# Index keys projected ahead of the index queries, a row ring of six, and an output projection prepared in the block before it

## The chip, the core and the metric

The kernel runs on one core of a Trainium2 chip. Its engines work from instruction streams of their own: TensorE (PE, matrix products), VectorE (DVE), ScalarE (ACT), GpSimd (POOL) and SyncE (SP, which here only issues transfers). Semaphores order them against each other. The metric is the device time of one execution in microseconds (us).

## The reference, cut to what matters

One inference step of one decoder layer, for a prompt of 1024 tokens and 8 samples of 4 tokens, with D_MODEL = 1024:

```python
mod = silu(c) @ w_ada + b_ada                       # six vectors per sequence: sh1, sc1, g1, sh2, sc2, g2
xn = rms_norm(x, norm1_g) * (1 + sc1) + sh1
qa, ka, va, qb, kb, vb, iq, ik, iw = split_proj(xn @ w_in)
# q, k of both mixers: rms_norm and rotary; iq, ik: rotary only
oa = combine_patterns(dilated attention of 8 heads under three (window, dilation) patterns)
I = sum_h iw[:, h] * relu(iq[:, h] @ ik.T)          # 8 index heads of 64
sel = top_k(I, 256 causal keys per query);  ob = softmax attention of 8 heads over sel
x = x + g1 * (concat(oa, ob) @ w_out)
xn = rms_norm(x, norm2_g) * (1 + sc2) + sh2
y = x + g2 * ((silu(gate) * up) @ w_down)           # gate, up = split(xn @ w_gate_up)
```

## The kernel before

The program is four blocks in sequence; all engines meet at the end of each: `front` (norm, modulation, input projection, index scores, top-k search), `attention` (prompt), `sample_attention` (the samples' attention) and `back` (output projection, second norm, FFN). Tokens stand in columns in three thirds of 352 (1024 + 32 samples), or in nine tiles of rows (eight of 128 and one of 32). Products in fp32 are made in three passes: a high and a low part of each operand (whi, wlo of the weights, xhi, xlo of the normed input), as hi x hi, hi x lo and lo x hi, each a group of eight matmuls over the depth of 1024. ACT writes the high parts, POOL the low parts of weights, DVE those of x.

**Projection.** `project` takes a chunk of up to 256 columns of w_in and runs its nine units (one for each row tile). The index chunks stand first (CH, L307: iq, iq, ik), then the index scores (`indexer`), then nine late chunks (LATE, L308: qa, qa, ka, ka, kv, qb, qb, va, va). The key chunk ik of 128 columns is projected the other way round, into three thirds (L613, 72 products in all), copied out by ACT as ikF, and turned into nine row tiles (L634); ACT copies out each tile's keys (ikn) and head weights (iw), POOL rotates them. Then come `kk` (the keys rounded, ACT L903) and `ll` (their remainder, POOL L1106), PE's transposes of both (L686), and `turn_queries` (L691) for each head. A pass over x starts with DVE's normed xnorm (L1217 to L1233) and its remainder xlo (L1237).

**Late chunks.** ACT's `unit` (L836) copies a unit out of PSUM into a row of `ubuf`, a ring of four, and sums squares per head; `root` (L830) takes the root of the sum of the unit before; DVE scales the row (L1442), POOL rotates it, and SP stores it to memory. A row is free once its store has landed (L851). Between units DVE runs the search for the top-k thresholds, for which ACT makes some of the counts (`tally`). After each of the late chunks except the last, two pieces of the modulation are multiplied (`ada`, L576, eight matmuls of 32 x 256 each); ACT copies each to modn (L809), and `ada_turn` (L590) turns it with two small matmuls behind units 0 and 1 of the next chunk. All engines keep the order in which their code is written.

**Sample attention and back.** `sample_attention` loads window keys kw (8 loads of 512 KB; consts after the first), turns them, ACT and DVE copy them out as kTa (ACT L2148), and so on to PE's last transposes of the result into oT (L2137). `back` then loads the output weights ow (SP `load_out` L2309), ACT rounds oT to ahi (L2473) and ow to owh (L2469), POOL makes owl (L2555), DVE makes alo (L2604), and PE multiplies (L2387).

Of the kernel before, what the change touches and what calls it, by code (L numbers as in the profile page):

```python
# [32 lines left out]
P = 128  # L33
# [27 lines left out]
XB = 25344  # L61

# [132 lines left out]
def front(nc, A, S):  # L195
# [5 lines left out]

    rope = T.at("rope", [P, NTILE + 1, 32], F32, S["pers"])
# [13 lines left out]
    ss = T.at("ss", [P, 4, 4], F32, T.end)  # L216
    sd = T.at("sd", [P, 4, 4], F32, T.end)
    rs = T.at("rs", [P, 4, 4], F32, T.end)
# [23 lines left out]
    ubuf = T.at("ubuf", [P, 4, WCH], F32, UB)  # L242
    usq = T.at("usq", [P, 4, WCH], BF16, T.end)
# [21 lines left out]
    sco = T.at("sco", [P, sum(width)], F32, T.end)  # L265
    relu = T.at("relu", [P, 2, 1024], F32, WB)
    kk = T.at("kk", [P, NTILE, 2, HD], F32R, T.end)
    ll = T.at("ll", [P, NTILE, 2, HD], F32R, T.end)
    qst = T.at("qst", [P, 2, 6, 2, HD], F32R, T.end)
    assert T.end <= WB + 24 * KD * P  # L270
# [36 lines left out]
    CH = [("iq", IQ, 256), ("iq", IQ + 256, 256), ("ik", PROJ - P, P)]  # L307
# [29 lines left out]
    LOAD_AT = 7  # L337
    FIRST_SPLIT_AT = 4
# [51 lines left out]
    tot = [0] * 4  # L390
    for u in range(NIDX, len(units)):
        tot[u % 4] += len(stores(u))
        nst[u] = tot[u % 4]
# [38 lines left out]
    unit_st = [sem(f"unit_st{r}") for r in range(4)]  # L432
# [41 lines left out]
    with nc.Block() as block:  # L474

        @block.sync
        def _(sp):
# [29 lines left out]
            def store(u):  # L507
# [6 lines left out]
                for s in stores(u):  # L514
                    if len(s) == 4:
                        n = s[3]
                        src = ubuf[n * TSEQ:(n + 1) * TSEQ, u % 4, s[1]:s[2]]
                    else:
                        src = ubuf[0:rows, u % 4, s[1]:s[2]]
                    sp.dma_start(s[0], src).then_inc(unit_st[u % 4], 16)  # L520
# [21 lines left out]
        def _(pe):  # L542
# [58 lines left out]
            def project(n, turns=()):  # L601
# [5 lines left out]
                if order[n][0] == "ik":  # L607
                    pe.wait_ge(sx_ev, 2)

                    for th in range(3):  # L610
                        for p, (a, b) in enumerate(((whi, xhi), (wlo, xhi), (whi, xlo))):
                            for k in range(KD):
# [4 lines left out]
                for t in range(NTILE + 1):  # L617
                    u = c * (NTILE + 1) + t
                    if c == 0:
                        th = min(2, (t * P + P - 1) // THIRD)  # L620
                        pe.wait_ge(xhi_done, KD * (th + 1) + (th == 2))
                    if t == 0:
                        pe.wait_ge(ada_nat, ada_at)
                        pe.wait_ge(ada_done, ada_at)
# [12 lines left out]
                    for p, (a, b) in enumerate(((xhi, whi), (xhi, wlo), (xlo, whi))):  # L637
                        if c == 0 and p == 2:
                            pe.wait_ge(xlo_done, KD * (th + 1) + (th == 2))
# [4 lines left out]
                    if t < len(turns):  # L644
                        ada_turn(turns[t])
# [31 lines left out]
            def indexer():  # L677

                pe.wait_ge(ada_done, ada_at)
                for x in range(4):  # L680
                    src, ready = ((kk, 1), (ll, 2))[x // 2]
                    pe.wait_ge(ik_split, ready)
                    if x >= 2:
                        wait_out(pe, x - 2)
# [6 lines left out]
                def turn_queries(h):  # L691
                    pe.wait_ge(iq_hi, h + 1)
                    pe.wait_ge(iq_lo, h + 1)
                    for part in range(2):
                        x = 4 + 2 * h + part
                        wait_out(pe, x - 2)
                        for j in range(4 if part == 0 else 2):
                            mm = pe.transpose(bank[2 + x % 2][:, j * P:(j + 1) * P],
                                              qst[:, h % 2, 4 * part + j].rearrange("p a d -> p (a d)").bitcast(F32),
                                              ident[:])  # L700
                        mm.then_inc(tr_fill, 1)

                turn_queries(0)
# [89 lines left out]
        def _(act):  # L793
# [36 lines left out]
            def root(u):  # L830
                if u >= 0 and normed(u):
                    act.wait_ge(unit_read, u + 1)
                    act.activation(sd[:, u % 4, 0:heads(u)], ss[:, u % 4, 0:heads(u)], ACT.Sqrt,
                                   scale=1.0 / HD, bias=EPS).then_inc(sd_ready, 1)

            def unit(u):  # L836
# [12 lines left out]
                else:  # L849
                    if u - NIDX >= 4:  # L850
                        act.wait_ge(unit_st[u % 4], 16 * nst[u - 4])  # L851
                    last = act.activation(ubuf[:, u % 4, :], src[:, 0:256], ACT.Copy)
                    if normed(u):
                        for h in range(heads(u)):
                            cols = slice(h * HD, (h + 1) * HD)
                            last = act.activation(usq[:, u % 4, cols], src[:, cols], ACT.Square,
                                                  accum_out=ss[:, u % 4, h:h + 1])
# [29 lines left out]
            act.wait_ge(x_spilt, 16)  # L887
            for u in range(9):
                unit(u)
            split_w(base + 2)  # L890
            for u in range(9, 18):
                unit(u)
            for th in range(3):
                act.wait_ge(ikf_mm, th + 1)
                act.activation(ikF[:, th * THIRD:(th + 1) * THIRD],
                               wide[th // 2][:, 512 * (th % 2):512 * (th % 2) + THIRD], ACT.Copy).then_inc(ikf_out, 1)
            for u in range(18, 27):
                unit(u)


            act.wait_ge(unit_rope, rope_before[NIDX])
            act.wait_ge(unit_mm, NIDX)
# [1859 lines left out]
```

## Time and profile before

| | us |
|---|---|
| median of 3 runs (lowest to highest) | 1792.56 (1792.12 to 1794.27) |
| the profiled execution | 1792.48 |
| its span, first to last instruction | 1790.9 |
| PE busy | 1612.7 (90%) |
| DVE, ACT, POOL busy | 868.3, 684.2, 587.3 |

The mean clock that TensorE was granted is 0.954 of full speed. Where the chunks of the projection, the index scores and the blocks lie in the span is read from lines of code: index chunks 72 to 145 us, index scores 158 to 219, late chunks 219 to 522, `attention` to 828, `sample_attention` to 881, `back` to the end. A row of the timeline gives a start, a duration, the engine, the line, what is written and read, how many instructions stand together, and in brackets the idle time ahead of it with what ended it. In rows of waits the columns are total, times and longest.

### The profile page before, as it was taken

What the parts mean: (1) busy time and instruction counts of PE and PEld (TensorE: products, weight loads), DVE (VectorE), ACT (ScalarE), POOL (GpSimd) and SP (SyncE); (2) the same over time, 40 slices, a digit from 0 to 9 for tenths busy, and PEclk for the clock granted to TensorE, in tenths of its full rate; (3) what the DMA queues carried; (4) which work ended last, traced back from release to release, by engine and by line L of the source; (5) the groups of instructions that cost most, each with busy time, mean ns of one, the idle gap of its engine ahead of it and who ended that gap; (6) DMA issues with size and microseconds to landing.
All of it is one profiled execution on the core that took longest, in us unless ns stands there. A gap on an engine that the chain in (4) does not pass through costs nothing.

```text
span 1790.9 us, 29669 instructions
## 1 busy us (share of the span) xinstructions
PE 1612.7 (90%) x10750; PEld 1515.3 (85%) x10750; DVE 868.3 (48%) x1995; ACT 684.2 (38%) x1780; POOL 587.3 (33%) x741
## 2 busy tenths in 40 slices
PE   5696898999888888886699699999999999999998
PEld 3594688888877777775499599999999999999998
DVE  1904977877778888885521731321312313303214
ACT  4414647667437778773322511111121121121111
POOL 2344155646423433212124233232232132232220
PEclk7798999999989999998799899999999999999999
DMA  7700033443342221103530221121011111111002
GB/s 253 260 25 6 25 99 102 129 152 102 111 144 70 86 69 58 38 8 115 218 115 13 66 75 48 36 59 47 23 51 43 47 47 47 47 47 35 12 1 98
DMA packets 138045, 135.30 MB, mean 76 GB/s; under 512 B 7229, under 2 KB 126957, under 8 KB 137302
## 3 DMA queue, kind: packets, MB, share of 16 engines
q1 hardware_dynamic: 111190, 106.43, 18.8%
q10 hardware_dynamic: 25104, 24.64, 4.3%
q0 software_dynamic: 1648, 2.89, 0.5%
q8 instruction: 59, 0.97, 0.2%
q14 instruction: 44, 0.36, 0.1%
HBM read 115.29 MB, written 27.04 MB: 79 GB/s over the span
## 4 chain that ended last, share of the span: by engine, by line
PE 48%; DVE 2%; DMA 1%; ACT 1%; POOL 0%; issue 0%; DVEq 0%; SPq 0%
PE bank L2408 28%; PE wide L2424 14%; PE bank L2387 5%; DVE xn L2647 0%; DVE alo L2657 0%; DMA out_y_p<-yn 0%; DVE rstd L2631 0%; DMA ow<-in_w_out 0%; ACT ahi L2524 0%; POOL owl L2555 0%; DVE yn L2701 0%; ACT gwh L2482 0%; PE wide L2369 0%; PE bank L2448 0%; ACT L2496 0%; ACT L2514 0%
## 5 line engine op out<-in xcount | busy, mean ns | idle before, releaser
L2668 DVE TENSOR_TENSOR hf<-bank,sg 128x352 f32<-128x352 f32 x66 | 34.7, 525 | 463.7 <-PE bank L2408 454.5
L2569 POOL TENSOR_TENSOR hlo<-hf,hhi 128x352 fp32r<-128x352 f32 x66 | 62.7, 949 | 503.9 <-ACT hhi L2498 503.9
L2408 PE MATMUL bank<-ahi,gwh 128*128 128x352 f32 x1056 | 196.3, 328 | 11.5 <-DVE hf L2668 6.6
L2681 DVE SCALAR_TENSOR_TENSOR x<-wide,modT,x 128x352 f32<-128x352 f32 (+1 forms) x264 | 151.2, 573 | 97.0 <-PE wide L2424 97.0
L2408 PE MATMUL bank<-alo,gwh 128*128 128x352 f32 x1056 | 192.1, 324 | 2.3 <-DVE alo L2657 2.3
L2408 PE MATMUL bank<-ahi,gwl 128*128 128x352 f32 x1056 | 193.2, 325 | 0.0
L2408 PEld LDWEIGHTS bank<-ahi,gwh 128*128 128x128 f32 x1056 | 176.3, 190 | 14.3 <-DVE hf L2668 6.9
L2408 PEld LDWEIGHTS bank<-alo,gwh 128*128 128x128 f32 x1056 | 174.2, 189 | 2.9 <-DVE alo L2657 2.9
L2408 PEld LDWEIGHTS bank<-ahi,gwl 128*128 128x128 f32 x1056 | 175.9, 190 | 0.0
L2424 PE MATMUL wide<-hlo,dwh 128*128 128x352 f32 x528 | 171.3, 325 | 0.0
L2424 PE MATMUL wide<-hhi,dwl 128*128 128x352 f32 x528 | 170.4, 323 | 0.0
L2424 PE MATMUL wide<-hhi,dwh 128*128 128x352 f32 x528 | 170.0, 322 | 0.0
L2496 ACT ACTIVATE sg<-bank 128x352 f32<-128x352 f32 x66 | 30.7, 466 | 355.7 <-PE bank L2408 355.7
L2498 ACT ACTIVATE hhi<-hf 128x352 fp32r<-128x352 f32 x66 | 33.0, 500 | 255.9 <-DVE hf L2668 255.9
L2559 POOL TENSOR_TENSOR gwl<-gw,gwh 128x2048 fp32r<-128x2048 f32 x22 | 103.0, 4680 | 62.0 <-ACT gwh L2482 62.0
L1784 PE MATMUL bank<-ident,prob 128*128 128x128 f32 x576 | 97.0, 278 | 17.9 <-DVE pL L1924 17.0
L1924 DVE TENSOR_TENSOR pL<-bank,pH 128x512 fp32r<-128x512 f32 (+1 forms) x192 | 101.3, 551 | 13.4 <-ACT pH L1871 11.7
L1356 DVE TENSOR_SCALAR_CACHE_REDUCE junk<-sig,cand 128x384 uint8<-128x384 f32 (+4 forms) x155 | 106.3, 743 | 0.1
L1896 ACT ACTIVATE prob<-smx,nmax 128x128 f32<-128x128 f32 (+7 forms) x128 | 99.0, 773 | 10.3 <-DVE nmax L1954 9.6
L1871 ACT ACTIVATE pH<-bank 128x512 fp32r<-128x512 f32 (+1 forms) x192 | 90.4, 486 | 25.1 <-PE bank L1784 24.2
L2424 PEld LDWEIGHTS wide<-hhi,dwh 128*128 128x128 f32 x528 | 100.0, 189 | 0.0
L2424 PEld LDWEIGHTS wide<-hlo,dwh 128*128 128x128 f32 x528 | 99.2, 188 | 0.0
(349 smaller groups left out, 3449.1 us busy)
## 6 DMA issues: line engine op xcount, KB each, us to landing
gw<-in_w_gate_up SPq DMA_DIRECT2D x44, 512.0 KB, 5.0
raw<-in_w_ada ACTq DMA_DIRECT2D x14, 1024.0 KB, 6.3
dw<-in_w_down SPq DMA_DIRECT2D x22, 512.0 KB, 3.6
raw<-in_w_ada SPq DMA_DIRECT2D x10, 1024.0 KB, 7.5
raw<-in_w_in ACTq DMA_DIRECT2D x8, 1024.0 KB, 5.4
scr_x<-xT SPq DMA_DIRECT2D x1, 4224.0 KB, 18.6
xnat<-in_x_prompt SPq DMA_DIRECT2D x8, 512.0 KB, 5.8
scr_q<-ubuf SPq DMA_DIRECT2D x32, 128.0 KB, 1.8
```

The lines of the kernel that those rows point to most:

```text
L1356: link(v.tensor_scalar(junk[0:r, joff[a]:joff[a] + w], sig[0:r, o:o + w], cand[0:r, a:a + 1].bitcast(F32), 0.0, ALU.is_ge, ALU.add, accum_ ...
L1784: mm = pe.transpose(dst[:, (j - 4 * b) * P:(j - 4 * b + 1) * P], prob[:, a % RING, j * P:(j + 1) * P], ident[:])
L1871: act.activation(pH[g][:, 4 * b:4 * b + nb, i % 4, :], src[:, 0:nb * P].rearrange("p (j n) -> p j n", n=P), ACT.Copy).then_inc(act_out, 1)
L1896: act.activation(prob[:, m % RING, 0:L], smx[:, m % 2, 0:L], ACT.Exp, scale=-1.0, bias=nmax[:, m % 4:m % 4 + 1], accum_out=rowsum[:, m // ...
L1924: v.tensor_tensor(pL[g][:, 4 * b:4 * b + nb, i % 4, :], src[:, 0:nb * P].rearrange("p (j n) -> p j n", n=P), pH[g][:, 4 * b:4 * b + nb, i ...
L2387: mm = pe.matmul(pb[u % 4][:, 0:THIRD], a[:, d % 2, k, :], b[:, k, third(th)], start=(p == 0 and k == 0), stop=(p == 2 and k == KD - 1))
L2408: mm = pe.matmul(pb[2 * s + side][:, 0:THIRD], a[r][:, k, side, :], b[:, k, third(th)], start=(p == 0 and k == 0), stop=(p == 2 and k == K ...
L2424: mm = pe.matmul(pb[4 + u % 4][:, 0:THIRD], a[:, r, d * P:(d + 1) * P], b[:, r, third(th)], start=(r == 0 and p == 0), stop=(r == 1 and p ...
L2559: pool.tensor_tensor(gwl[r][:], gw[r][:], gwh[r][:].bitcast(F32), ALU.subtract).then_inc(gw_lo, 1)
L2569: pool.tensor_tensor(hlo[:, r, third(th)], hf[:, (3 * r + th) % 2, :], hhi[:, r, third(th)].bitcast(F32), ALU.subtract).then_inc(h_lo, 1)
L2668: v.tensor_tensor(hf[:, s, :], pb[2 * s + 1][:, 0:THIRD], sg[:, s, :], ALU.mult).then_inc(h_mul, 1)
L2681: ins = v.scalar_tensor_tensor(out=x1[:, d, cols], in0=src[:, 0:n], scalar=modT[:, 40 + d, 0:1], in1=x1[:, d, cols], op0=ALU.mult, op1=ALU ...
```

## The change

Three parts.

First, CH becomes ik, iq, iq. The key chunk's products wait for xhi and xlo by thirds, as the first chunk's units did. The kk turns follow the first unit of the second iq chunk, the ll turns the third, and the first head's queries the seventh; they are in a buffer of their own, q0st. ACT makes kk after the fifth unit of the first iq chunk and POOL ll after its rotation; kk, ll and q0st move to where the scores will lie. In ACT and POOL the steps move with them.

Second, ubuf, ss, sd and rs have six rows (ROWS), and `ada_turn` and ACT's bias step stand behind units 3 and 4 (MOD_TURN_AT).

Third, `sample_attention` issues its constants ahead of the window keys, and takes over from `back`: the first two column blocks of ow are loaded, rounded (ACT) and split (POOL) there; ACT rounds two thirds of oT, two pieces after each kTa, and POOL makes their remainders (16 subtractions, olo in place on oT). `back` does the last third. It loads x first, and the down weights only after the output projection.

The core of the diff:

```diff
-    CH = [("iq", IQ, 256), ("iq", IQ + 256, 256), ("ik", PROJ - P, P)]
+    CH = [("ik", PROJ - P, P), ("iq", IQ, 256), ("iq", IQ + 256, 256)]
+    ROWS = 6
-    ubuf = T.at("ubuf", [P, 4, WCH], F32, UB)
+    ubuf = T.at("ubuf", [P, ROWS, WCH], F32, UB)
+    MOD_TURN_AT = 3
...
                     for th in range(3):
+                        pe.wait_ge(xhi_done, KD * (th + 1) + (th == 2))
                         for p, (a, b) in enumerate(((whi, xhi), (wlo, xhi), (whi, xlo))):
+                            if p == 2:
+                                pe.wait_ge(xlo_done, KD * (th + 1) + (th == 2))
...
-                    if t < len(turns):
-                        ada_turn(turns[t])
+                    if 0 <= t - MOD_TURN_AT < len(turns):
+                        ada_turn(turns[t - MOD_TURN_AT])
+                    if c == 2 and t in (0, 2):
+                        turn_keys(t // 2)
+                    if c == 2 and t == 6:
+                        turn_queries(0)
...
-                    if u - NIDX >= 4:
-                        act.wait_ge(unit_st[u % 4], 16 * nst[u - 4])
+                    if u - NIDX >= ROWS:
+                        act.wait_ge(unit_st[u % ROWS], 16 * nst[u - ROWS])
...
-                        if turns:
+                        if turns and t >= MOD_TURN_AT:
                             ada_bias(turns.pop(0))
...
+            sp.wait_ge(sc, 2)
+            for d in range(2):
+                sp.dma_start(ow[:, d], A["w_out"][0, :, d * P:(d + 1) * P].rearrange("(k p) n -> p k n", p=P)
+                             ).then_inc(ow_in[d], 16)
...
+            for th in range(2):
+                for k in range(KD):
+                    pool.wait_ge(o_hi, KD * th + k + 1)
+                    pool.tensor_tensor(olo[:, k, third(th)], oT[:, k, third(th)], ahi[:, k, third(th)].bitcast(F32),
+                                       ALU.subtract).then_inc(o_lo, 1)
+            for d in range(2):
+                pool.wait_ge(ow_hi, d + 1)
+                pool.tensor_tensor(owl[:, d], ow[:, d], owh[:, d].bitcast(F32), ALU.subtract).then_inc(ow_lo, 1)
...
+                for k in (2 * (n % 4), 2 * (n % 4) + 1):
+                    act.activation(ahi[:, k, third(n // 4)], oT[:, k, third(n // 4)], ACT.Copy).then_inc(o_hi, 1)
...
-            load_out(0)
-            load_out(1)
             for g, (k0, k1) in enumerate(XG):
                 sp.dma_start(x1[:, k0:k1], A["scr_x"][:, k0:k1]).then_inc(x_in[g], 16)
             load_out(2)
             load_out(3)
 
-            sp.wait_ge(o_hi, 3 * KD)
-            sp.wait_ge(o_lo, 3 * KD)
             load_gate_up(0, 0)
-            load_down(0, 0)
-            load_down(1, 1)
             for d in range(4, KD):
                 load_out(d)
             sp.wait_ge(op_mm, 3 * KD)
             load_gate_up(1, 1)
+            load_down(0, 0)
+            load_down(1, 1)
```

PE around the index chunks, before: the last unit of the second query chunk, the key chunk's last third (L613) and its turns (L634), then the turns of kk, ll and the queries (L686, L698) and the first score (L719).

```order
L641 MATMUL bank<-whi,xlo 128x256 x8
...
L613 MATMUL wide<-xlo,whi 128x352 x8
L634 MATMUL bank<-ident,ikF 128x128 x8
L634 MATMUL bank<-ident,ikF 32x128
L686 MATMUL bank<-ident,kk 128x128 x8
L686 MATMUL bank<-ident,ll 128x128 x8
L698 MATMUL bank<-ident,qst 128x128 x6
L719 MATMUL wide<-ikH,iqT 128x384
```

PE now: the key chunk (L624) stands first, its turns (L639) next, and the turns of kk, ll (L691) and q0st (L704) lie between units (L644) of the second query chunk.

```order
L624 MATMUL wide<-xlo,whi 128x352 x8
L639 MATMUL bank<-ident,ikF 128x128 x8
L639 MATMUL bank<-ident,ikF 32x128
L644 MATMUL bank<-whi,xhi 128x256 x8
...
L691 MATMUL bank<-ident,kk 128x128 x8
...
L691 MATMUL bank<-ident,ll 128x128 x8
...
L704 MATMUL bank<-ident,q0st 128x128 x6
...
L726 MATMUL wide<-ikH,iqT 128x384
```

The turns moved from behind the last product to between products; the first score follows the last unit.

PE at the start of the second late chunk, before: the two pieces of the modulation (L586), a unit of three groups (L641), and behind it the first turn (L597).

```order
L586 MATMUL bank<-raw,cT 32x256 x16
L641 MATMUL bank<-whi,xhi 128x256 x8
L641 MATMUL bank<-wlo,xhi 128x256 x8
L641 MATMUL bank<-whi,xlo 128x256 x8
L597 MATMUL wide<-modsel,modn 128x9 x2
```

PE now, at the same place: four units (L644) stand between the pieces (L592) and the first turn (L603).

```order
L592 MATMUL bank<-raw,cT 32x256 x16
L644 MATMUL bank<-whi,xhi 128x256 x8
L644 MATMUL bank<-wlo,xhi 128x256 x8
...
L644 MATMUL bank<-wlo,xhi 128x256 x8
L644 MATMUL bank<-whi,xlo 128x256 x8
L603 MATMUL wide<-modsel,modn 128x9 x2
```

The turn moved back by three units.

POOL at the end of the samples' block and the start of the next, before: the last gather of values (vpg), the change of block, and the remainders of four blocks of ow.

```order
L2050 DMA vpg<-in_cache_v 128x128
L2021 UNCONDITIONAL_BRANCH
L2550 UNCONDITIONAL_BRANCH
L2555 TENSOR_TENSOR owl<-ow,owh 128x1024 x4
L2579 TENSOR_TENSOR sqsum<-sqsum,sq_13638 128x352 x3
```

POOL now, from the last gather on: 16 remainders of oT and two of ow stand ahead of the change of block.

```order
L2088 DMA vpg<-in_cache_v 128x128
L2094 TENSOR_TENSOR olo<-oT,ahi 128x352 x16
L2098 TENSOR_TENSOR owl<-ow,owh 128x1024 x2
L2056 UNCONDITIONAL_BRANCH
L2585 UNCONDITIONAL_BRANCH
L2590 TENSOR_TENSOR owl<-ow,owh 128x1024 x2
```

Half of the first four owl moved into the samples' block, behind sixteen new subtractions.

## Rows read from the trace of the kernel before

**Rows 1.** The page: chain that ended last, shares of the span by line.

```profile
PE bank L2408 28%; PE wide L2424 14%; PE bank L2387 5%; DVE xn L2647 0%; DVE alo L2657 0%; DMA out_y_p<-yn 0%; DVE rstd L2631 0%; DMA ow<-in_w_out 0%; ACT ahi L2524 0%; POOL owl L2555 0%; DVE yn L2701 0%; ACT gwh L2482 0%; PE wide L2369 0%; PE bank L2448 0%; ACT L2496 0%; ACT L2514 0%
```

**Rows 2.** Windows: late chunks, samples; PE, PEld, DVE, ACT, POOL busy, clock, DMA.

```profile
219.00:522.00 303.00, 278.07 (x2324) 265.82 (x2323) 237.74 (x661) 179.34 (x803) 155.40 (x333) 0.94 0.36 115
829.00:889.00 60.00, 37.63 (x316) 24.59 (x315) 26.11 (x81) 12.76 (x28) 12.05 (x20) 0.74 0.60 203
```

**Rows 3.** Timeline of PE, index chunks and the turns behind them.

```profile
86.44 1.12 PE L641 MATMUL bank<-whi,xlo 128*128 128x256 f32 x8
87.40 1.12 PE L641 MATMUL bank<-whi,xhi 128*128 128x256 f32 x8
...
140.81 1.44 PE L613 MATMUL wide<-xlo,whi 128*128 128x352 f32 x8
...
145.13 0.29 PE L634 MATMUL bank<-ident,ikF 128*32 128x128 f32 x1 [0.19 <-ACT iw L847]
151.42 1.94 PE L686 MATMUL bank<-ident,kk 128*128 128x128 f32 x8 [6.01 <-ACT kk L903]
```

**Rows 4.** Timeline of DVE, first normed pieces and the last of xlo.

```profile
66.83 4.62 DVE L1217 TENSOR_TENSOR xnorm<-xnorm,sc 128x256 f32<-128x256 f32 x1
71.49 0.43 DVE L1220 TENSOR_TENSOR xnorm<-xnorm,modT 128x256 f32<-128x256 f32 x1
...
90.83 1.01 DVE L1237 TENSOR_TENSOR xlo<-xnorm,xhi 128x320 fp32r<-128x320 f32 x2
```

**Rows 5.** Timeline of ACT: the first relu of the index scores.

```profile
158.38 1.07 ACT L939 ACTIVATE relu<-wide 128x384 f32<-128x384 f32 x2 [0.45 <-PE wide L719]
```

**Rows 6.** Waits of PE, late chunks (218 to 522 us).

```profile
PE wide L597 <- ACT modn L809: 21.0, 6, 5.6
PE bank L586 <- ACT modn L809: 3.5, 1, 3.5
```

**Rows 7.** Waits of ACT on stores of the row ring, same stretch.

```profile
ACT ubuf L852 <- DMA scr_q<-ubuf: 23.2, 6, 6.7
ACT ubuf L852 <- DMA out_win_k_p<-ubuf: 13.9, 5, 4.9
```

**Rows 8.** Timeline of PE, a late chunk: a wait and what follows.

```profile
292.19 1.02 PE L597 MATMUL wide<-modsel,modn 128*128 128x9 f32 x4 [4.72 <-ACT modn L809]
293.06 2.05 PE L641 MATMUL wide<-whi,xhi 128*128 128x256 f32 x8
294.91 1.91 PE L641 MATMUL wide<-wlo,xhi 128*128 128x256 f32 x8
```

**Rows 9.** Waits of DVE, late chunks.

```profile
DVE rs L1439 <- ACT sd L833: 38.1, 21, 3.5
DVE nok L1363 <- ACT tally L969: 19.6, 14, 4.6
```

**Rows 10.** Chain that ended last, output projection: start, duration, what.

```profile
881.10 4.12 DMA ow<-in_w_out
...
885.24 1.07 ACT owh L2469
...
886.38 2.35 POOL owl L2555
```

**Rows 11.** Timeline of PE, samples' block and start of the output projection.

```profile
835.48 2.28 PE L2070 MATMUL bank<-mask_sb,expand 32*128 32x288 f32 x4 [5.86 <-DMA headsel<-in_headsel]
...
888.82 2.68 PE L2387 MATMUL bank<-ahi,owh 128*128 128x352 f32 x8 [8.45 <-POOL owl L2555]
```

**Rows 12.** The page's groups: a POOL subtraction of 128x352 (busy, mean ns).

```profile
L2569 POOL TENSOR_TENSOR hlo<-hf,hhi 128x352 fp32r<-128x352 f32 x66 | 62.7, 949 | 503.9 <-ACT hhi L2498 503.9
```

**Rows 13.** Timeline of DVE, samples' block: the first scaling of pr_s.

```profile
860.07 0.37 DVE L2196 TENSOR_SCALAR pr_s<-pr_s,rsum_s 128x288 f32<-128x288 f32 x1
```

**Rows 14.** Lines L1442 and L1042, late chunks: ns min/median/max.

```profile
L1442 DVE TENSOR_TENSOR ubuf<-ubuf,rs x63: 291/426/2389, 227.7 to 467.6; 128x256 f32<-128x256 f32 x54, 128x128 f32<-128x128 f32 x9
...
L1042 POOL TENSOR_TENSOR wlo<-raw,whi x16: 2397/2411/2588, 237.2 to 479.7; 128x1024 fp32r<-128x1024 f32 x16
```

More of the change, by code:

```diff
@@ L689, in indexer, with turn_queries @@
                     mm.then_inc(tr_fill, 1)
[L691 to L703, printed above, removed]
+            def turn_queries(h):
+                pe.wait_ge(iq_hi, h + 1)
+                pe.wait_ge(iq_lo, h + 1)
+                src = q0st if h == 0 else qst[:, h % 2]
+                for part in range(2):
+                    x = 4 + 2 * h + part
+                    wait_out(pe, x - 2)
+                    for j in range(4 if part == 0 else 2):
+                        mm = pe.transpose(bank[2 + x % 2][:, j * P:(j + 1) * P],
+                                          src[:, 4 * part + j].rearrange("p a d -> p (a d)").bitcast(F32),
+                                          ident[:])
+                    mm.then_inc(tr_fill, 1)
+            def indexer():
                 n = 0
@@ L886, in _ @@
                                    bias=modT[:, k, 0:1]).then_inc(xhi_done, 1)
[L887 to L902, printed above, removed]
-            act.activation(kk[:], ikn[:, 0:NTILE, :].unsqueeze(2).to_broadcast([P, NTILE, 2, HD]),
-                           ACT.Copy).then_inc(ik_split, 1)
             def iq_high(h):
@@ L1102, in _ @@
             split_w(base + 2)
-            for u in range(9, NIDX):
+            for u in range(9, 9 + 5):
                 rotate(u)
@@ L1995, in sample_attention @@
     rsum = T.at("rsum_s", [P, 4], F32, T.end)
+    kw = T.at("kw", [P, 3, KT, 512], F32, T.end)
+    assert T.end <= OW, T.end
+    kTa = T.at("kTa", [P, 4, 4, NEWW], F32, T.end)
+    kTb = T.at("kTb", [P, 4, NEWW], F32, T.end)
+    assert T.end <= S["loaded"]
+    ow = T.at("ow", [P, 2, KD, P], F32, OW)
+    owh = T.at("owh", [P, 2, KD, P], F32R, T.end)
+    owl = T.at("owl", [P, 2, KD, P], F32R, T.end)
+    T.end = OW
     n_pool = A["cache_k"].shape[1]
@@ L2019, in sample_attention, with third @@
     xt = sem("s_o_turned")
+    ow_in = [sem(f"b_ow_in{r}") for r in range(2)]
+    o_hi = sem("b_o_hi")
+    o_lo = sem("b_o_lo")
+    ow_hi = sem("b_ow_hi")
+    ow_lo = sem("b_ow_lo")
+    S.update(ahi=ahi, olo=olo, ow=ow, owh=owh, owl=owl, ow_in=ow_in, o_hi=o_hi, o_lo=o_lo, ow_hi=ow_hi, ow_lo=ow_lo)
+    def third(t):
+        return slice(t * THIRD, (t + 1) * THIRD)
     with nc.Block() as block:
@@ L2153, in _ @@
                                accum_out=lsum[:, x:x + 1]).then_inc(ex, 1)
+            for d in range(2):
+                act.wait_ge(ow_in[d], 16)
+                act.activation(owh[:, d], ow[:, d], ACT.Copy).then_inc(ow_hi, 1)
         @block.vector
@@ L2229, in back @@
     OT = PERS_END
-    ahi = T.at("ahi", [P, KD, TOK], F32R, OT + 4 * KD * TOK)
-    xn = T.at("xn2", [P, KD, TOK], F32, T.end)
+    ahi, olo, ow, owh, owl = [S[x] for x in ("ahi", "olo", "ow", "owh", "owl")]
+    xn = T.at("xn2", [P, KD, TOK], F32, OT + 8 * KD * TOK)
     alo = T.at("alo", [P, KD, TOK], F32R, OT + 8 * KD * TOK)
@@ L2246, in back @@
     hf = T.at("hf", [P, 2, THIRD], F32, T.end)
-    ow = T.at("ow", [P, 2, KD, P], F32, GW + 24 * P * KD)
-    owh = T.at("owh", [P, 2, KD, P], F32R, T.end)
-    owl = T.at("owl", [P, 2, KD, P], F32R, T.end)
-    assert T.end <= SMALL
+    assert OW == GW + 24 * P * KD
     dw = T.at("dw", [P, 2, D], F32, OT)
@@ L2380, in _ @@
                         pe.wait_ge(x1_done, u - 3)
-                    for p, (a, b) in enumerate(((owh, ahi), (owl, ahi), (owh, alo))):
+                    for p, (a, b) in enumerate(((owh, ahi), (owl, ahi), (owh, olo))):
                         for k in range(KD):
@@ L2469, in split_out @@
                 act.activation(owh[:, d % 2], ow[:, d % 2], ACT.Copy).then_inc(ow_hi, 1)
-            for th in range(3):
-                for k in range(KD):
-                    act.activation(ahi[:, k, third(th)], oT[:, k, third(th)], ACT.Copy).then_inc(o_hi, 1)
-                if th == 0:
-                    split_out(0)
-                    split_out(1)
+            for k in range(KD):
+                act.activation(ahi[:, k, third(2)], oT[:, k, third(2)], ACT.Copy).then_inc(o_hi, 1)
             def split_gate_up(i, r, fresh):
@@ L2600, in _ @@
                                    op0=ALU.add, op1=ALU.mult).then_inc(op_link, 1)
[L2601 to L2605 removed]
+            for k in range(KD):
+                v.wait_ge(o_hi, KD * 2 + k + 1)
+                v.tensor_tensor(olo[:, k, third(2)], oT[:, k, third(2)], ahi[:, k, third(2)].bitcast(F32),
+                                ALU.subtract).then_inc(o_lo, 1)
             for d in range(KD):
```

143 lines of the change are left out of this document (79 added, 64 removed).

## The prediction, made before the changed kernel ran

> **What bounds the kernel now.** I read the chain that ended last first: its two largest lines, 28% and 14% of the span, are TensorE (PE) products of the back block [rows 1], which the change leaves as they are. A gain can only come from stretches where PE waits or runs at its lower clock. Two stand out in the stage windows: the projection chunks, 303 us with PE busy 278 and a granted clock of 0.94, and the attention of the samples, 60 us with PE busy 38 at a clock of 0.74 [rows 2]. A third is the step from the last projected index column to the first index score, which the timelines show as short transposes behind waits [rows 3, 5]. The change touches exactly these three; I cost it as A (index keys first), B (six rows, later turns of the modulation) and C (out projection prepared early).
>
> **A, index keys first.** Before, the key chunk comes last. Its last product ends at 142.25 [rows 3], and a serial chain follows: nine ikF transposes until 145.42, POOL's rotations of nine key tiles, ACT's kk, PE's turn of kk at 151.42 after a wait of 6.01, then ll and the queries, and ACT's first relu of a score at 158.38 [rows 3, 5]. That is 16.1 us behind the last product.
>
> After, I build the end up from the front. The key chunk runs in three thirds, and the last group of each needs eight xlo tiles of its third. VectorE (DVE) ends the last of them at 91.84 [rows 4]. Half as many columns make the first weight split of POOL half as long, which stood before DVE's first step (4.62 us, where the like step behind it takes 0.43 [rows 4]); I let the xlo chain end 2.5 us earlier, at 89.3 (bounds: 0 and 4). The last group of eight, 1.44 [rows 3], gives 90.8. The nine ikF transposes, 3.2 us (142.25 to 145.42), give 94.0. Two query chunks are 18 units of three groups that start 0.96 apart [rows 3], 2.88 each: 51.8, so 145.8. Between their units now stand the turns of kk (1.94 at about half clock [rows 3]), ll and six query transposes, which fall on the full clock: I take 2.5 for all, 148.3. None of them should wait: POOL has a whole chunk (26 us) for its nine key rotations, which took 7 us, and kk and ll behind them. What is left behind the last product is one query tile's copy and rotation, the second head's split and the first score with its relu: 2.5 (the last three are about 1.5 in the chain before; between 1.5 and 4). The first relu stands at 150.8 instead of 158.4: A = **-7.5**. With xlo not earlier and PE at its lower clock for the last third and the first unit after it (4 us), A = -1; with the best ends -10. The index scores go at a pace that DVE and ACT set, so what the first relu gains is passed on whole.
>
> **B, six rows, and the turns at units 3 and 4.** In the chunks PE waits 21.0 + 3.5 = 24.5 us for ACT's modn, the copy that ada_turn turns [rows 6]. ACT has it late because its in-order stream stands at the next unit's ubuf copy until a store of the row four units back has landed; the two larger groups of such waits are 23.2 and 13.9 us [rows 7]. A row's way is copy, squares, a root one unit later, DVE's scale, POOL's rotation, store. Four units are 11.5 us, and since ACT stands for it, the way takes somewhat more; six rows give 17.3. Independently the turn moves behind units 3 and 4, so modn has three more units, 8.6 us, where the longest wait is 5.6 [rows 6]. Either half by itself would cover most of it; both together leave nothing: -24.5.
>
> Each wait also drops the clock. After 4.72 us at 292.19 a group of eight takes 2.05 us against 1.12 [rows 3, 8]; such groups start 1.85 apart and not 0.96, and with three of them after each wait 2.7 us go. Of the seven waits one or two are short and cost less; I take 15.5 for all. B is at most -40. It doesn't have to come whole, since DVE searches the top-k thresholds in the same stretch and the block ends when both do. DVE is busy 237.7 of 303 us [rows 2] and waits 38.1 for ACT's sd and 19.6 for its tally [rows 9]. With PE's 40 us gone 263 are left: DVE would be busy 90%, and its waits would have to shrink from 58 to 25. Most should, since sd and tally are late for the reason that ACT is held, but not surely all; I give back 6. B = **-34**, between -16 (below) and -40. The store waits are ACT's alone, so nothing is queued behind them on another engine; the two added rows are 2 KB of each partition and take no time.
>
> **C, out projection prepared early.** The chain behind the samples' last transposes is: load of ow 4.12, ACT's owh 1.07, POOL's owl 2.35, and PE starts at 888.82 after 8.45 us [rows 10, 11]. After, ow, owh and owl of the first two column blocks and two thirds of ahi and olo are done inside the sample block, where ACT and POOL have little else, and PE starts at about 881.2: -7.6. The last third's eight ahi and olo are due only when PE has done two thirds, 7.7 us later, and are covered. The constants now precede the first key window: PE waited 5.86 us for the last of them [rows 11], issued behind 512 KB; -0.5. Added are 16 subtractions on POOL of about 0.95 each [rows 12], 15 us from the end of its gathers on, in which DVE's four scalings of pr_s (0.37 each [rows 13]) stand on PE's path. The row of 4.62 [rows 4] shows that POOL can hold DVE as long as its own operation lasts; a scaling that meets one loses up to 0.95, and I take two: +1.6. In the back x1 is loaded first and the down weights only behind the out projection. The down products come after a whole pair's gate and up products, over 20 us; I cost that at nothing (uncovered, one load and its split: 6 us). C = **-6.5**, between 0 and -8.5.
>
> The Trainium skill ("SBUF — State Buffer", section "Who interferes with whom") calls that pair of ports a lock: a VectorE operation in a two-port mode, or with two operands in SBUF against a GpSimd operation that reads SBUF, stands until the other is over. The trace agrees (4.62 against 0.43); by that rule POOL's new work could hold only the four scalings, 3.8 us at most, and not the copies out of PSUM around them.
>
> **The sum.** The profiled execution took 1792.48 us with a span of 1790.9; the median is 1792.56, so no correction. 1792.5 - 7.5 - 34 - 6.5 = **1744.5**.
>
> **Rivals.** (1) DVE sets the end of the projection. If its waits on ACT [rows 9] stay for the most part, because latency and not ACT's stall causes them, then PE waits at the end for DVE and little but what DVE spares comes back: B = -16, total 1762.5. For it: 90% busy is close. Against it: ACT's stalls are in the trace. (2) A gives little: the thirds wait for xlo at the lower clock, and the turns inside the second query chunk stand for kk, ll or the query split, each of which needs ACT and POOL in turn; A = -1, total 1751. (3) Half of B only: a new cause (tallies, splits) keeps modn late, B = -20, total 1758.5. (4) Slower than before: POOL and DVE bunch. A scale in the chunks takes 0.43 in the median and 2.39 at most, about as long as one of POOL's wlo splits (2.41) [rows 14]. If the closer stream sets the 54 full-size scales against POOL operations of that length, each takes 1.9 more, 103 us on DVE. DVE has 303 - 238 = 65 us, and A and C give 14: it decides from 79 / 1.9 = 42 of the 54 on, and at all of them the total is 1792.5 + 103 - 79 = 1816. Against it: there are only 16 such splits [rows 14], so POOL's short rotations would have to hold as long.
>
> **How the numbers follow.** The forecast and what lies within 8 us of it: 0.62. Rival 1: 0.14. Rival 3: 0.10. Rival 2: 0.09. Rival 4: 0.02. Several shortfalls at once, near no change: 0.03. The low end is A -10, B -39, C -8.5, or 1735; the high end takes in rivals 2, 3 and 1 with a little margin: 1765. A measurement of this kernel can tell about 0.2%, 3.6 us, from no change; all but 5 in 100 end below 1789.
>
> **What would show it.** A: the first relu at 151 instead of 158, and no 6 us wait before the kk turn. B: no wait for modn over 1 us, ACT's waits on stores under 10 us in all, the granted clock of the chunks at 0.99, and the chunks some 34 us shorter; if DVE's waits on sd stay near 38 instead, rival 1. C: the first product of the out projection within 1 us of the samples' last transpose, and no scaling of pr_s over 1 us. The prediction is wrong if the waits for modn vanish and the end of the projection doesn't come forward by over 20 us.

## The result, and the profile after

The changed kernel takes 1745.36 us in the median (1743.9 to 1747.06), the kernel before on the same chip 1793.41; the ratio is 0.9733, 95% interval 0.9716 to 0.9749. The forecast was 1744.5. The total fits within 1 us, but its three terms don't: by the two profiled executions two came out larger and one much smaller than forecast.

Where the 48.6 us of the two spans (1790.9 to 1742.3) lie, by the starts of the first instruction of each stage in the two traces:

| stage | before | after | gain |
|---|---|---|---|
| start to the first relu of the scores | 158.38 | 152.66 | 5.72 |
| first relu to the first product of the late chunks | 60.43 | 64.10 | -3.67 |
| late chunks, to the last product | 302.79 | 263.11 | 39.68 |
| step into `attention`, and that block | 307.06 | 308.05 | -0.99 |
| samples' block, to the first product of the output projection | 60.16 | 51.82 | 8.34 |
| the rest | 902.1 | 902.6 | -0.5 |

The windows of the changed kernel, for the late chunks, the scores and the samples' block. The columns are length, busy time of PE, its weight loads, DVE, ACT and POOL, the granted clock, and DMA.

```profile
216.76:479.87 263.11, 262.36 (x2326) 252.02 (x2324) 239.64 (x662) 177.91 (x802) 155.95 (x333) 1.00 0.41 132
152.66:216.76 64.10, 48.34 (x212) 34.13 (x212) 54.16 (x54) 40.81 (x63) 16.20 (x10) 0.89 0.02 5
787.92:839.74 51.82, 36.74 (x318) 24.00 (x318) 24.31 (x72) 15.41 (x35) 28.70 (x36) 0.80 0.63 210
```

Against [rows 2]: in the late chunks PE is busy for all but 0.75 us, at the full clock, and DVE is busy for about as long as it was. That is all that the chunks can give while PE does these products. The waits of the same stretch, answering [rows 6, 7, 9] (total, times, longest):

```profile
PE bank L592 <- ACT modn L816: 0.7, 1, 0.7
...
ACT ubuf L859 <- DMA out_win_k_p<-ubuf: 0.9, 1, 0.9
...
DVE rs L1457 <- ACT sd L840: 10.7, 9, 2.6
DVE nok L1381 <- ACT tally L977: 4.2, 5, 1.4
```

The waits for modn fell from 24.5 to 0.7, ACT's waits on stores to 0.9, and DVE's two waits on ACT from 57.7 to 14.9. The chunks end with PE's last product and DVE's last write of the search. The two are level here (479.87 and 479.78), and they were in the kernel before (521.60 and 522.08), so a gain needed both to come earlier. Their rows, before and then after:

```profile
520.56 1.04 PE L660 MATMUL bank<-ident,lst 128*128 128x128 f32 x8
521.78 0.30 DVE L1417 TENSOR_SCALAR mask_sb<-sig 32x288 f32<-32x288 f32 x1
...
478.83 1.04 PE L667 MATMUL bank<-ident,lst 128*128 128x128 f32 x8
479.48 0.30 DVE L1435 TENSOR_SCALAR mask_sb<-sig 32x288 f32<-32x288 f32 x1
```

The start, on PE (answering [rows 3]): the last group of the keys' third, which waits for xlo; the end of the nine turns; the first two groups of queries; the turns between the units; the first score.

```profile
89.96 1.55 PE L624 MATMUL wide<-xlo,whi 128*128 128x352 f32 x8 [2.29 <-DVE xlo L1256]
...
94.39 0.28 PE L639 MATMUL bank<-ident,ikF 128*32 128x128 f32 x1 [0.20 <-ACT iw L854]
94.67 1.64 PE L644 MATMUL bank<-whi,xhi 128*128 128x256 f32 x8
96.10 1.91 PE L644 MATMUL bank<-wlo,xhi 128*128 128x256 f32 x8
...
125.02 1.03 PE L691 MATMUL bank<-ident,kk 128*128 128x128 f32 x8
131.64 1.04 PE L691 MATMUL bank<-ident,ll 128*128 128x128 f32 x8
144.02 0.82 PE L704 MATMUL bank<-ident,q0st 128*128 128x128 f32 x6
...
150.42 0.34 PE L726 MATMUL wide<-ikH,iqT 128*128 128x384 f32 x1
```

No turn waits, as forecast; three turns cost 2.9 (2.5 forecast). The first unit of queries takes 4.4 us from 94.67 to 99.10 where a unit at the full clock takes 2.88.

The scores are where the gain was lost. DVE, POOL and PE in the third head, each from the timeline of that engine:

```profile
169.05 6.78 DVE L1288 SCALAR_TENSOR_TENSOR sco<-relu,iw,sco 128x384 f32<-128x384 f32 x3 [1.31 <-ACT relu L947]
```

```profile
168.72 4.51 POOL L1044 TENSOR_TENSOR wlo<-raw,whi 128x2048 fp32r<-128x2048 f32 x1 [7.11 <-ACT whi L835]
```

```profile
174.59 1.51 PE L704 MATMUL bank<-ident,qst 128*128 128x128 f32 x6 [4.62 <-issue]
175.76 0.78 PE L726 MATMUL wide<-ikH,iqT 128*128 128x512 f32 x1
```

POOL splits the weights of the first late chunk in the middle of the scores. DVE's step stands for as long, PE idles for 4.62 us and goes on at the lower clock (six turns in 1.51 us, against 0.82 above). The kernel before has the same stall, so it was no news of the change; but there PE was back at the full clock by the fourth head, and in this execution of the changed kernel it was not. The windows of that head, of the changed kernel, of the kernel before, and of e1 (below), whose code is the changed kernel's up to there:

```profile
181.96:190.19 8.23, 7.11 (x27) 5.22 (x27) 6.78 (x8) 5.13 (x10) 1.69 (x1) 0.79 0.00 0
```

```profile
185.26:192.25 6.99, 5.76 (x27) 3.84 (x27) 6.75 (x8) 5.02 (x9) 1.69 (x1) 1.00 0.00 0
```

```profile
181.70:188.68 6.98, 5.75 (x27) 3.83 (x27) 6.74 (x8) 5.02 (x10) 1.70 (x1) 1.00 0.00 0
```

So of the 3.67 us 1.2 lie in this head, 1.1 in the third by the same cause (13.42 against 12.31), and 1.3 in the first (7.60 against 6.30), where PE's turn of the second head's queries stands until POOL has made their remainder, which comes behind two transfers of keys (it ends at 155.16):

```profile
155.26 0.84 PE L704 MATMUL bank<-ident,qst 128*128 128x128 f32 x6 [1.17 <-issue]
```

```profile
152.49 0.96 POOL L1130 DMA_DIRECT2D out_ik_p<-ikn  x1 [0.30 <-POOL iqn L1094]
153.45 0.52 POOL L1131 DMA_DIRECT2D out_ik_s<-ikn  x1
153.98 1.18 POOL L1106 TENSOR_TENSOR qst<-iqn,qst 128x384 fp32r<-128x384 f32 x1
```

Only the loss in the first head belongs to the new order. In e1 to e4, which have the changed kernel's code up to there, the first head takes 7.61 to 9.73 us, the third 12.42 to 13.41 and the fourth 6.98 to 7.04; in e8, with the old order, these are 6.30, 13.15 and 6.99. What the third and fourth head lost here differs from execution to execution.

The samples' block: the output projection starts 0.92 us behind the change of block and waits for nothing else (8.45 before, [rows 11]), but one scaling of pr_s takes 2.37 us instead of 0.37 [rows 13], and PE waits for it:

```profile
819.22 2.37 DVE L2247 TENSOR_SCALAR pr_s<-pr_s,rsum_s 128x288 f32<-128x288 f32 x1
```

```profile
807.15 14.28 POOL L2094 TENSOR_TENSOR olo<-oT,ahi 128x352 fp32r<-128x352 f32 x16
```

```profile
821.65 1.35 PE L2159 MATMUL bank<-ident,pr_s 128*128 128x128 f32 x6 [3.82 <-DVE pr_s L2247]
...
839.74 2.68 PE L2426 MATMUL bank<-ahi,owh 128*128 128x352 f32 x8 [0.92 <-PEq L2056]
```

The scaling ends at 821.59, POOL's run of 16 subtractions at 821.43. From that turn of pr_s to the end of the block's last transposes this execution had more of the full clock than the kernel before and the other runs that leave POOL's run whole. The windows of that stretch, before, after, and in e2 (below):

```profile
860.49:880.37 19.88, 17.83 (x140) 9.86 (x140) 6.30 (x18) 0.41 (x2) 0.00 (x0) 0.70 0.21 75
```

```profile
821.65:838.82 17.17, 15.56 (x140) 7.71 (x140) 6.31 (x18) 2.12 (x2) 4.70 (x2) 0.80 0.36 103
```

```profile
817.97:837.70 19.73, 18.33 (x140) 8.39 (x140) 6.30 (x18) 2.12 (x2) 4.67 (x2) 0.67 0.25 65
```

### The profile page after: what moved, and what is told of

It is laid out like the page before. It is cut to its first block, busy times and chain, and to the rows that moved or that the text cites. A ratio compares the mean times of both kernels' runs of the same rounds, so it can differ in the third digit from the quotient of the medians.

```text
span 1742.3 us, 29645 instructions
## 1 busy us (share of the span) xinstructions
PE 1596.6 (92%) x10750; PEld 1502.3 (86%) x10750; DVE 862.1 (49%) x1979; ACT 682.0 (39%) x1780; POOL 601.2 (35%) x757
## 4 chain that ended last, share of the span: by engine, by line
PE 49%; DVE 2%; ACT 1%; DMA 0%; issue 0%; DVEq 0%; ACTq 0%; SPq 0%
PE bank L2447 29%; PE wide L2463 15%; PE bank L2426 5%; DVE xn L2681 0%; DVE alo L2691 0%; DVE rstd L2665 0%; DMA out_y_p<-yn 0%; ACT ahi L2559 0%; PE bank L2487 0%; ACT gwh L2517 0%; PE wide L2408 0%; DVE yn L2735 0%; ACT L2531 0%; ACT L2549 0%; ACT yn L2583 0%
## 5 line engine op out<-in xcount | busy, mean ns | idle before, releaser
L1914 ACT ACTIVATE prob<-smx,nmax 128x128 f32<-128x128 f32 (+7 forms) x128 | 98.7, 771 | 10.4 <-DVE nmax L1972 9.7
L2463 PEld LDWEIGHTS wide<-hhi,dwl 128*128 128x128 f32 x528 | 99.2, 188 | 0.0
```

Source lines behind the costliest of these rows:

```text
L1914: act.activation(prob[:, m % RING, 0:L], smx[:, m % 2, 0:L], ACT.Exp, scale=-1.0, bias=nmax[:, m % 4:m % 4 + 1], accum_out=rowsum[:, m // ...
L2463: mm = pe.matmul(pb[4 + u % 4][:, 0:THIRD], a[:, r, d * P:(d + 1) * P], b[:, r, third(th)], start=(r == 0 and p == 0), stop=(r == 1 and p ...
```

## The experiments

All start from the changed kernel. Its own time is 1745.36. A ratio in brackets is to the kernel before on the same chip, with its 95% interval; the changed kernel's own is 0.9733 (0.9716 to 0.9749).

**e1_ring4 and e2_turn0: which half of B does it?** e1 takes the ring back to four rows, e2 the turns back to units 0 and 1.

```diff
-    ROWS = 6                      (e1)
+    ROWS = 4
-    MOD_TURN_AT = 3               (e2)
+    MOD_TURN_AT = 0
```

> The changed kernel with the row ring back at four rows; the turns of the modulation stay behind units 3 and 4. Theory 1 (each half of B alone covers the modn waits): no wait for modn over 1 us, since the turn has 8.6 us more than before and the longest wait was 5.6; ACT's waits on stores stay near 40 us but hold nobody; 1745 to 1750 us. Theory 2 (the ring is what counts, since ACT that stands for a store also makes sd and tally late for VectorE): PE still stalls in the chunks, for ACT's unit copies or at the end of the search, and the time is 1760 to 1775 us.

> The changed kernel with the turns of the modulation back behind units 0 and 1; the ring stays at six rows. Theory 1 (each half alone covers the modn waits): waits for modn of 0 to 5 us in all, 1745 to 1752 us. Rival (ACT's copy of modn is late for other reasons than the stores): six waits of some 2 us, each with its stretch at the lower clock, 1765 to 1772 us.

e1 took 1766.55 us (ratio to before 0.9847, 0.9829 to 0.9864), e2 1743.28 (0.9712, 0.9696 to 0.9728). So the ring by itself brings all that B brings, and the turns add nothing that can be measured to it. The turns by themselves are worth something, but not most. The windows of the chunks, e1 and then e2:

```profile
215.20:504.20 289.00, 268.82 (x2326) 257.24 (x2324) 239.89 (x662) 177.96 (x803) 157.41 (x333) 0.97 0.38 120
```

```profile
214.90:478.00 263.10, 262.32 (x2325) 251.98 (x2324) 239.00 (x661) 178.08 (x802) 156.65 (x333) 1.00 0.41 132
```

In e1 the later turns do what was said of them: one wait for modn is left, of 3.6 us, ahead of the products of the modulation and not of their turn. But ACT still stands for the stores, and what it makes for DVE comes late; PE stands 10.4 us more in six places ahead of units, where the profile names ACT for 2.3 of it and nothing for the rest. The waits of e1, ACT's first, then DVE's:

```profile
ACT ubuf L859 <- DMA scr_q<-ubuf: 28.1, 9, 6.0
...
ACT ubuf L859 <- DMA out_win_k_p<-ubuf: 16.4, 6, 4.2
...
ACT ubuf L859 <- DMA out_v_p<-ubuf: 9.3, 3, 4.0
```

```profile
DVE rs L1457 <- ACT sd L840: 28.0, 19, 2.8
DVE nok L1381 <- ACT tally L977: 13.1, 12, 2.0
```

ACT's waits are 53.8 us and DVE's 41.1, and the stretch now ends with DVE: its last write of the search comes at 504.2, PE's last product of the chunks at 498.0. That is rival 1 of the prediction, in the kernel that keeps the short ring.

```profile
496.97 1.04 PE L667 MATMUL bank<-ident,lst 128*128 128x128 f32 x8
503.90 0.30 DVE L1435 TENSOR_SCALAR mask_sb<-sig 32x288 f32<-32x288 f32 x1
```

**e3_keys_and_out: both halves undone.**

```diff
-    ROWS = 6
+    ROWS = 4
-    MOD_TURN_AT = 3
+    MOD_TURN_AT = 0
```

> The changed kernel with both halves of B undone (four rows, turns behind units 0 and 1): the index keys first and the early output projection alone. By the two traces the chunks gave 39.7 of the 48.6 us, so 1785 us, with modn waits of about 24 us back. If the parts lean on each other (the chunks start 2 us earlier, the stores lie otherwise), 1775 to 1780.

1780.77 us (0.9919, 0.9903 to 0.9936), 35.4 above the changed kernel: between the two expectations. Its stretch from the last relu of the scores to the first product of `attention` takes 303.8 us, 3.6 less than before (307.4), at nearly the same waits for modn (24.2):

```profile
PE wide L603 <- ACT modn L816: 20.6, 6, 5.0
PE bank L592 <- ACT modn L816: 3.6, 1, 3.6
```

So the stalls of a ring that is too short can move by some us between two kernels whose code for the stretch is the same; why was not tested. With that, the same stretch can be set side by side for the four kernels: short ring and early turns 303.8, short ring and late turns 291.0, long ring and early turns 267.7, long ring and late turns 267.6.

**e4_pool_after_scaling: is the long scaling POOL's doing?**

```diff
                 for k in range(KD):
+                    if th == 1 and k == 4:
+                        pool.wait_ge(nr, 4)
                     pool.wait_ge(o_hi, KD * th + k + 1)
```

> The changed kernel, where POOL makes 12 of its 16 subtractions in the samples' block, then waits until VectorE has scaled pr_s four times, and makes the last four and the two of ow after that. Theory (the one scaling of 2.37 us is VectorE held by POOL's run of subtractions): that scaling takes 0.37, the samples' block ends 2 us earlier, 1743.4 us. Rival (the scaling is long for another reason, or what it holds is not on the path): 1745.4 us, no change.

1742.94 us (0.9716, 0.97 to 0.9732); by the time alone that is not apart from 1745.36. The trace is clearer: the first scaling takes 1.18 us, since it meets the last of the 12 subtractions, and the next three 0.37.

```profile
817.39 1.18 DVE L2249 TENSOR_SCALAR pr_s<-pr_s,rsum_s 128x288 f32<-128x288 f32 x1
```

```profile
807.66 10.74 POOL L2096 TENSOR_TENSOR olo<-oT,ahi 128x352 fp32r<-128x352 f32 x12
```

The scaling ends at 818.57, POOL's 12 at 818.40. In e2, where nothing of the block was changed, the scaling met the run earlier and took 3.64; it again ended with the run (817.92 and 817.75):

```profile
814.28 3.64 DVE L2247 TENSOR_SCALAR pr_s<-pr_s,rsum_s 128x288 f32<-128x288 f32 x1
```

```profile
803.47 14.28 POOL L2094 TENSOR_TENSOR olo<-oT,ahi 128x352 fp32r<-128x352 f32 x16
```

The same scaling took 3.8 in e1, 3.7 in e3 and e5, 4.0 in e6 and 4.2 in e8. Where DVE comes upon the run does not matter to PE, since the scaling ends with the run: PE's turn of pr_s starts 33.7 us after the block's first product in all seven kernels that leave the run whole, 30.2 in e4 and 29.6 in e7, so the run costs 3.5 to 4.1 us. The block from its first product to the first of the output projection takes 54.4 to 54.7 in e1 to e3, e5, e6 and e8, 50.8 in e4, and 51.8 in the changed kernel's own profile, which is the shorter one only behind that turn, at a clock of 0.80 where the six have 0.66 or 0.67. So C is worth 5.5 to 5.8 us by six executions and 8.3 by one; why the clock differed there was not settled.

**e5_split_early: is it the split on POOL that spoils the scores?** ACT's and POOL's split of the first late chunk moves from the second and third head to behind the first unit of the second query chunk. ACT's wait for the turns of the keys ahead of it goes with that.

```diff
...
             for u in range(18, 27):
                 unit(u)
+                if u == 18:
+                    split_w(pj[0])
...
-                if h == EARLY_SPLIT:
-                    split_w(pj[0])
...
             for u in range(9 + 5, 18 + 3):
                 rotate(u)
+                if u == 18:
+                    split_w(ns[0])
...
-                if h == EARLY_SPLIT:
-                    split_w(ns[0])
```

> The changed kernel, where the weights of the first late chunk are split (ACT 1.9 us, POOL 4.5 us) behind the first unit of the second query chunk and no longer behind the second head of the index scores; POOL is free there now that the key rotations have moved, and VectorE idle. Theory (POOL's 4.5 us holds VectorE's score step for as long, PE idles for 4.6 us and then runs at its lower clock for one to two heads): the scores take 56 to 58 us instead of 64, no score step over 2 us, clock 1.00 throughout, 1737 to 1739 us. Rival (the heads have a pace of 7 us and the split only fills what would be waited for anyway): scores of 62 us or more, 1743 to 1746 us.

1735.03 us (0.968, 0.9649 to 0.9711). The scores take some 56 us, a head 6.97 to 6.99 from the third to the sixth, and no score step is long any more. Both splits were moved at once: the second head, which held ACT's, falls from 8.28 to 6.45, the third, which held POOL's, from 13.42 to 6.97. The line of DVE's score steps (min, median, max in ns), first of the changed kernel, then of e5:

```profile
L1288 DVE SCALAR_TENSOR_TENSOR sco<-relu,iw,sco x42: 614/1084/4589, 160.8 to 217.1; 128x384 f32<-128x384 f32 x7, 128x512 f32<-128x512 f32 x7, 128x640 f32<-128x640 f32 x7, 128x768 f32<-128x768 f32 x7
```

```profile
L1288 DVE SCALAR_TENSOR_TENSOR sco<-relu,iw,sco x42: 610/1014/1361, 160.0 to 206.8; 128x384 f32<-128x384 f32 x7, 128x512 f32<-128x512 f32 x7, 128x640 f32<-128x640 f32 x7, 128x768 f32<-128x768 f32 x7
```

**e6_head1_early: the second head's queries.**

```diff
-            act.wait_ge(unit_rope, rope_before[NIDX])
             n = 0
...
                 if h + 1 < 8:
+                    if h == 3:
+                        act.wait_ge(unit_rope, rope_before[NIDX])
                     iq_high(h + 1)
...
             for u in range(18 + 3, NIDX):
+                if u == NIDX - 1:
+                    iq_low(1)
                 rotate(u)
...
-                if h:
+                if h > 1:
                     iq_low(h)
```

> The changed kernel, where ACT rounds the second head's queries right behind the last unit's copy, without waiting for all rotations (that wait moves ahead of the fifth head), and POOL makes their remainder ahead of the last rotation and the two transfers of the keys. Theory (of the first relu's 152.66, 1.2 us is the wait for POOL's rotation, and the second head's queries then come late): first relu about 1.2 us earlier, the first head 6.3 to 7 us instead of 7.6, 1743.5 us. Rival (later heads take it back): 1745 us.

1739.31 us (0.9707, 0.9677 to 0.9737); by the time alone that is not apart from the changed kernel. The first relu stands at 149.70, 3.0 earlier (1.2 expected; in the kernels with the code of the changed one up to there it stands between 151.7 and 154.2, so the rest may be no more than that spread), and the first head takes 6.29. The third and fourth take 12.6 and 7.0: the stall is there, but PE is back at the full clock in time, as in e1 to e4.

**e8_queries_first: part A undone** (queries, queries, keys, and the turns behind them; the other two parts kept).

```diff
-    CH = [("ik", PROJ - P, P), ("iq", IQ, 256), ("iq", IQ + 256, 256)]
+    CH = [("iq", IQ, 256), ("iq", IQ + 256, 256), ("ik", PROJ - P, P)]
...
             def indexer():
+                pe.wait_ge(ada_done, ada_at)
+                turn_keys(0)
+                turn_keys(1)
+                turn_queries(0)
...
```

> The changed kernel with the order of the index chunks undone: queries, queries, keys, and all turns behind the last product, as before; ring of six, turns at unit 3 and the early output projection stay. By the traces the first relu came 5.7 us earlier and the first late chunk only 2.1 us: so 1747 to 1748 us. Rival (the forecast: what the first relu gains is passed on): 1751 to 1753 us.

1748.81 us (0.9753, 0.9722 to 0.9784): 3.5 above the changed kernel, but the interval allows for no difference and for the 7.5 of the forecast alike. The trace says more. Its first relu is at 158.85, 6.2 later than in the changed kernel; its last at 219.4, 3.4 later (1.7 to 5.3 later than in the changed kernel and e1 to e4). So what the first relu gains was not passed on whole.

**e7_all: the three repairs together** (e5, e6, and e4 with the break after ten subtractions).

> The changed kernel with three edits: the early split of e5_split_early, the earlier second head of e6_head1_early, and POOL's subtractions of the samples' block broken off after ten until VectorE has scaled pr_s. If the three stretches are independent: 1745.4 - 7 - 2 - 3 = 1733 to 1735 us. Where the lower clock only moves to the next stretch, 1738 to 1741.

1729.07 us (0.9646, 0.9617 to 0.9674), faster than both kernels: 16 below the changed one, and more than the sum that was expected. Its scores and samples' block:

```profile
150.92:204.20 53.28, 44.69 (x212) 30.25 (x211) 49.12 (x54) 38.90 (x62) 13.47 (x13) 1.00 0.03 6
774.20:823.40 49.20, 36.54 (x317) 25.20 (x317) 22.18 (x72) 15.37 (x35) 28.75 (x36) 0.84 0.67 222
```

The scores are 10.8 shorter than in the changed kernel, at the full clock throughout; the samples' block is 2.6 shorter; the first relu comes 1.7 earlier. That is 15.2 of the 15.8 by which the spans differ. All four scalings now take 0.37:

```profile
L2252 DVE TENSOR_SCALAR pr_s<-pr_s,rsum_s x4: 369/370/370, 803.4 to 804.8; 128x288 f32<-128x288 f32 x4
```

## Why the prediction came out right, point by point

**A: forecast 7.5, the traces gave 2.05, undoing it cost 3.5, which is within the noise.** The step that failed is the last sentence of that part: "The index scores go at a pace that DVE and ACT set, so what the first relu gains is passed on whole." The first relu itself came at 152.66 for 150.8. Of the 1.9 us, 0.6 is the end of xlo (89.9 for 89.3) and about 1.5 the first query unit at the lower clock, which stood in the bound and not in the sum. Three quarters of the term were right, then. But behind the relu the heads keep DVE's and ACT's pace only where POOL is in time and leaves DVE alone. The new order starts the scores before POOL is through with the keys' transfers, so PE waits in the first head for the second head's remainder: 7.60 to 9.73 us in the five kernels with this code, 6.30 in both with the old order (before and e8), 6.29 where the remainder comes earlier (e6, e7). The trace of before also held DVE's score step of 4.6 us and PE's idle time behind it; it was read as part of a fixed pace. What the clock after that stall cost the changed kernel in the fourth head stands in its one execution and in none of the other runs, and why was not settled. So A is uncertain by some us: the first late product came at 214.85 to 218.47 in the five kernels, and at 218.81 and 220.15 with the old order.

**B: forecast 34 (at most 40), the traces gave 39.7.** Both terms held: modn waits 24.5 to 0.7, clock 0.94 to 1.00. What was wrong is the 6 given back for DVE: its waits on ACT fell to 14.9, below the 25 that had to be reached. The reason given, that sd and tally are late because ACT is held, was right. The sentence "Either half by itself would cover most of it" was right of the ring and wrong of the turns: e1 lost 21 us. It followed ACT's lateness to one consumer, PE, and the later turns free only that one; the longer ring removes the lateness and so serves DVE too.

**C: forecast 6.5, the traces gave 8.3, and 5.5 to 5.8 in e1 to e3.** The 7.6 of the chain were right: PE starts 0.92 us behind the change of block. Of the 8.3, 2.7 are the clock behind PE's turn of pr_s in the one execution (17.17 us for 19.88 before; 19.7 to 20.1 in e1 to e3, e5, e6 and e8), a term that stood nowhere in the sum. The price of the collision was mis-sized in kind: the bound was 0.95 for each scaling that meets a subtraction, two of them 1.6 to 1.9. In fact one scaling was held, until POOL's whole run was over, 2.0 to 3.8 us too long, and PE's turn of pr_s came 3.5 to 4.1 us later than where the run was broken off. The constants brought the product behind them forward by 0.6 us in the changed kernel (6.26 us after the block's first product, 6.82 before) and by 1.5 to 2.8 in the others, for the 0.5 of the forecast; where the run is whole this is lost again, since that turn then starts at 33.7.

The total was right because A's 5.5 us too many and 1.5 that went in `attention` and behind the output projection's start nearly cancel against the 7.5 by which B and C were put too low. That they cancel is luck, and the more so as A and C differ by some us between executions.

**The rivals.** Rival 1 (DVE sets the end) came about in e1 and not in the changed kernel, where DVE and PE end level; e1's stretch is 16.4 us shorter than before (291.0 for 307.4), close to the 16 that the rival gave without a sum. Rival 2 (A gives little) is what happened, at some 2 to 3.5 us, but elsewhere than it said: no turn waited, and the loss lay in the scores. Rival 4 had the right mechanism and the wrong place: the chunks' scales stayed at 0.43 in the median and 2.31 at most; POOL's long runs bite in the scores and in the samples' block.

The Trainium skill ("SBUF — State Buffer", section "Who interferes with whom") says that whoever takes the shared ports holds them "for the whole instruction". The traces of these runs show the loser standing for longer, to the end of a run of instructions that follow each other without a gap (below); the list of what collides in the Trainium skill fits the case, as only the scalings stood and not the copies out of PSUM beside them. In the trace of before another DVE step did get in at the seam between two splits of POOL (below).

## What to carry to other kernels

If an in-order engine stands for a buffer, lengthen the ring before moving its consumers: the longer ring serves every consumer of that engine, the later consumer only itself. Before passing a gain on through a stage with a fixed pace, look for the one long step in that stage and ask which engine holds it, and check whether an earlier start still finds everything that the stage needs. And new work for POOL belongs where VectorE has nothing to do between two SBUF tiles, or has to be broken off with a wait: for a step like the scaling of pr_s the price was not the length of one POOL instruction but that of its run without a gap. Last, compare one profiled execution with others of the same code before a difference of 1 us in a stage is put down to the change.

## What the runs showed of the hardware

One VectorE scaling of 0.37 us that met a run of POOL subtractions of about 0.9 us each stood through several of them until the run ended: 2.37 to 4.21 us in the seven kernels that leave the run whole, each time ending 0.16 or 0.17 us behind it, and 1.18 in e4, where the run was one subtraction from its end. That scaling was not let in between two instructions. It doesn't hold for every VectorE step: in the trace of before a small scalar_tensor_tensor that met the first of two back-to-back splits, of 4.5 us each, ended at 66.80, where the second began (66.7), and not with the second (71.17).

```profile
62.20 8.97 POOL L1035 TENSOR_TENSOR wlo<-raw,whi 128x2048 fp32r<-128x2048 f32 x2 [27.95 <-ACT whi L828]
...
64.48 2.32 DVE L1210 SCALAR_TENSOR_TENSOR sc<-modT,vecT 128x72 f32<-128x72 f32 x1
```

An idle time of 4.0 to 4.6 us of PE in the scores was followed by a granted clock of 0.62 over the third head and 0.79 over the fourth in the changed kernel, by 0.72 and 1.00 in the kernel before, and by 0.60 to 0.73 and 1.00 in e1 to e4, e6 and e8. Without it (e7) the clock is 1.00 in all eight heads.
